# A transformer layer on one core: the first stage in another order, with column sums in place of row sums and twenty identity matmuls at the start

## The reference, cut to what matters

```python
mod = silu(c) @ w_ada + b_ada                      # 1024 -> 6 x 1024
sh_a, sc_a, g_a, sh_f, sc_f, g_f = split(mod)
h = layer_norm(x) * (1 + sc_a) + sh_a              # x: 512 x 1024
na_q, na_k, na_v, d_q, d_k, d_v = split(h @ w_in)  # 1024 -> 6 x 512
mix = concat(neighbourhood_attention(na_q, na_k, na_v, na_rpb),    # 8 heads
             diff_attention(d_q, d_k, d_v, t5_bias, lambdas)) @ w_out  # 4 heads
x = layer_norm(alpha * x + (1 + g_a) * mix, ln1)
h = layer_norm(x) * (1 + sc_f) + sh_f
f = peer(h)      # 8 heads x 16 experts a token: rows gathered from expert_down, expert_up
x = layer_norm(alpha * x + (1 + g_f) * f, ln2)
```

## Time and profile before

| | us |
|---|---|
| median of 3 runs (1943.44 to 1948.09) | 1945.46 |
| the profiled execution, its own time | 1944.35 |
| its span, first to last instruction | 1942.6 |
| first projection matmul starts | 96.47 |
| last projection copied out, attention starts | 269.15 |
| first gather of both kinds | 609.38 |

### The profile page before, as it was taken

One profiled execution on the slowest core, in us unless ns is written; L12 is line 12 of the kernel. 1 busy time (PEld: TensorE's weight loads), 2 busy tenths in 40 slices (PEclk: granted clock), 3 DMA queues, 4 the chain that ended last, 5 costly groups with the idle time before them and its releaser, 6 DMA issues.

```text
span 1942.6 us, 14972 instructions
## 1 busy us (share of the span) xinstructions
PE 1537.7 (79%) x4570; PEld 687.8 (35%) x4570; DVE 1178.0 (61%) x2808; ACT 388.6 (20%) x955; POOL 984.3 (51%) x1065
## 2 busy tenths in 40 slices
PE   2599999999998777777777777777777777777777
PEld 1244446655996222222222222222222222222222
DVE  1844027758801677666777766776766776676642
ACT  1100025520112111221111221111321111221111
POOL 0000000000303777777777777777777777777772
PEclk9999989999998999999999999999999999999999
DMA  4965443022504999999999999999999999999994
GB/s 139 343 249 211 131 129 74 14 109 87 196 1 155 409 409 409 409 410 409 409 410 409 407 409 408 409 402 406 407 405 404 408 405 403 410 404 409 406 409 185
DMA packets 193334, 612.95 MB, mean 316 GB/s; under 512 B 30248, under 2 KB 30632, under 8 KB 192968
## 3 DMA queue, kind: packets, MB, share of 16 engines
q0 software_dynamic: 147456, 536.94, 69.6%
q1 hardware_dynamic: 45800, 75.06, 11.9%
HBM read 605.77 MB, written 6.16 MB: 315 GB/s over the span
## 4 chain that ended last, share of the span: by engine, by line
PE 25%; DMA 25%; DVE 24%; POOL 15%; issue 7%; SPq 2%; ACT 1%; POOLq 0%; DVEq 0%; PEldq 0%
DMA big<-in_expert_down,expert_idx 24%; PE pair L441 22%; DVE big L926 9%; POOL big L419 8%; POOL big L410 8%; PE pair L560 2%; SPq L295 1%; DMA big<-in_expert_up,expert_idx 1%; DVE big L733 1%; PE pair L504 1%; DVE big L863 1%; DVE big L846 1%; DVE big L867 1%; DVE big L868 1%; PE pair L544 1%
## 5 line engine op out<-in xcount | busy, mean ns | idle before, releaser
L560 PE MATMUL pair<-big 128*128 128x512 f32 x2048 | 999.9, 612 | 323.1 <-DMA big<-in_expert_up,expert_idx 288.4
L926 DVE CUSTOM_DVE_ANT_0 big<-big,pair 128x1024 f32<-128x1024 f32 x512 | 611.2, 1219 | 340.8 <-DMA big<-in_expert_down,expert_idx 339.5
L560 PEld LDWEIGHTS pair<-big 128*128 128x128 f32 x2048 | 349.0, 189 | 973.3 <-issue 858.3
L410 POOL DMA_INDIRECT big<-in_expert_down,expert_idx x512 | 484.7, 947 | 300.7 <-issue 119.9
L419 POOL DMA_INDIRECT big<-in_expert_up,expert_idx x512 | 483.6, 944 | 156.9 <-issue 147.1
L441 PE MATMUL pair<-big 128*128 128x128 f32 (+3 forms) x1704 | 421.9, 415 | 21.6 <-DVE big L733 13.2
L441 PEld LDWEIGHTS pair<-big 128*128 128x128 f32 (+2 forms) x1704 | 237.2, 193 | 166.1 <-issue 147.8
L398 POOL TENSOR_SCALAR small<-small 128x1 f32<-128x1 f32 (+1 forms) x16 | 3.6, 226 | 463.6 <-DVE small L806 350.7
L636 ACT ACTIVATE big<-big 128x16 f32<-128x16 f32 x32 | 6.9, 215 | 1026.0 <-DVE big L926 1026.0
L647 ACT ACTIVATE big<-ident,big 128x128 f32<-128x128 f32 x512 | 153.0, 387 | 16.1 <-DVE big L881 16.1
L629 ACT ACTIVATE big<-pair 128x512 f32<-128x512 f32 (+1 forms) x136 | 77.9, 591 | 323.1 <-PE pair L441 227.0
(11 more groups left out here) (111 smaller groups left out, 662.4 us busy)
## 6 DMA issues: line engine op xcount, KB each, us to landing
big<-in_w_ada SPq DMA_DIRECT2D x12, 2048.0 KB, 17.6
big<-in_w_in SPq DMA_DIRECT2D x6, 2048.0 KB, 15.5
big<-na_scr SPq DMA_DIRECT2D x8, 1024.0 KB, 10.6
big<-in_w_query SPq DMA_DIRECT2D x4, 2048.0 KB, 12.8
big<-in_expert_down,expert_idx POOLq DMA_INDIRECT x512, 11.8
big<-in_expert_up,expert_idx POOLq DMA_INDIRECT x512, 11.9
big<-in_w_out SPq DMA_DIRECT2D x2, 2048.0 KB, 10.6
x_sb<-in_x SPq DMA_DIRECT2D x1, 2048.0 KB, 7.9
```

The costliest lines, as they stand in the source:

```text
L410: nc.gpsimd.indirect_dma_start(downs[at % DOWN_SLOTS], None, expert_down[0], bass.IndirectOffsetOnAxis(expert_idx[:, at:at + 1], 0)).then_ ...
L560: last = nc.tensor.matmul(pair[t % 2][:, s * HALF:(s + 1) * HALF], diag[:, at % TOPK, :], ups[:, at % UP_SLOTS, s * HALF:(s + 1) * HALF], ...
L926: v.tensor_tensor_reduce(out=downs[slot], in0=downs[slot], in1=u_cur[:, :], scale=1.0, scalar=0.0, op0=ALU.mult, op1=ALU.add, accum_out=do ...
```

## The change

It rewrites the first stage and leaves the rest as it is.

- SP starts c, the first 2048 values of the bias `b_ada` and `na_rpb` first, each as plain rows, then x, the tables and the keys, and at once five weight chunks; the lambda vectors and `subln` come behind these. PE transposes the rows (groups `cols`, `rpb_cols`) and DVE copies them out.
- PE begins with twenty matmuls of the identity with itself (`WARM`).
- DVE takes the statistics of all four tiles in a row, POOL the power for all four in one instruction; ACT writes the normalised tiles.
- Scale and shift are applied after the transpose, where they are one number for each partition: `h_act` and `h_dve` are eight groups, one for each 128 columns of x, emptied by ACT (3) and DVE (5) with scale and shift in the same instruction.
- So ada 0 to 3 need not be put on all partitions: `mod_columns` turns each sum into columns by matmuls with one column of `ones`. Of chunks 2 and 3 POOL sums three of the eight blocks (`sum_blocks`), in `tensor_scalar` and `tensor_tensor`.
- `t5_line` becomes two groups in place of eight (the four heads share one matmul) and goes, with `keys_t`, behind the first projection. The projections come in the order 2, 5, 3, 4, 0, 1.
- The transfers to `na_scr` and `t5_scr` (the latter in four parts) stand behind the load of chunk 9.

```diff
+IN_ORDER = [2, 5, 3, 4, 0, 1]
+WARM = 20
+ADA_ON_DVE = [KB, KB, 5, 5]
...
-    g += [("t5_line", (h, s)) for h in range(DIFF_HEADS) for s in range(2)]
-    g += [("keys_t", ())]
-        if n == ADA_FIRST - 1:
-            g += [("h_t", (t, s)) for t in range(TILES) for s in range(2)]
+    g = [("cols", ()), ("rpb_cols", ())]
+    g += [("na_table", (j,)) for j in range(8)]
+    g += [("h_act" if k % 3 == 1 else "h_dve", (k,)) for k in range(KB)]
+        if n == 0:
+            g += [("t5_line", (s,)) for s in range(2)]
+            g += [("keys_t", ())]
...
+            for n in range(WSLOTS, WSLOTS + 3):
+                load_chunk(n)
+            for n in range(WSLOTS + 3, WSLOTS + 5):
+                load_chunk(n)
             sp.wait_ge(act_evac, EVAC[INDEX[("na_table", (7,))]][1])
             sp.dma_start(bass.AP(na_scr, 0, [[GRID_W, NA_HEADS * RPB_R], [NA_HEADS * RPB_R * GRID_W, GRID_W],
...
+            def sum_blocks(n):
+                pool.wait_ge(w_in_slot[n], 16)
+                acc, w, k0 = pool_sum[:, n % 2, :], w_slot[n], ADA_ON_DVE[n]
+                link(nc.gpsimd.tensor_scalar(acc, w[:, k0, :], c_exp[:, k0:k0 + 1], None, ALU.mult))
+                for k in range(k0 + 1, KB):
+                    link(nc.gpsimd.tensor_scalar(pool_tmp, w[:, k, :], c_exp[:, k:k + 1], None, ALU.mult))
+                    last = nc.gpsimd.tensor_tensor(acc, acc, pool_tmp, ALU.add)
...
+            def mod_columns(n):
+                pe.wait_ge(ada_summed, n + 1)
+                if ADA_ON_DVE[n] < KB:
+                    pe.wait_ge(pool_summed, sum(k < KB for k in ADA_ON_DVE[:n + 1]))
+                for b in range(4):
+                    last = nc.tensor.matmul(mod_ps[:, 4 * n + b:4 * n + b + 1], first_sum[:, n, b * P:(b + 1) * P],
+                                            ones[:, 0:1], start=True, stop=(ADA_ON_DVE[n] == KB))
...
+            for _ in range(WARM):
+                nc.tensor.matmul(spare_bank[:, 0:P], ident[:, :], ident[:, :], start=True, stop=True)
...
+                if kind == "h_dve" and args[0] == 6:
+                    for n in range(ADA_FIRST):
+                        last = mod_columns(n)
+                    last.then_inc(mod_summed, 1)
...
+                if kind == "na_table" and args[0] == 4:
+                    act.wait_ge(shift_ready, 1)
+                    for t in range(TILES):
+                        nc.scalar.activation(x_norm[:, t, :], x_sb[:, t, :], ACT.Identity, bias=shift4[:, t:t + 1],
+                                             scale=rstd4[:, t:t + 1]).then_inc(norm_ready, 1)
...
+                    v.tensor_scalar(h_t[:, k, :], ps[:, :], mod_cols[:, KB + k:KB + k + 1], mod_cols[:, k:k + 1],
+                                    ALU.mult, ALU.add).then_inc(dve_evac, 1)
```

More of the change, by code:

```diff
@@ L101 @@
 INDEX = {g: i for i, g in enumerate(GROUPS)}
-ON_DVE = ("ada", "scores", "values", "out")
+ON_DVE = ("cols", "rpb_cols", "h_dve", "ada", "scores", "values", "out")
 def at_head(a, head):
@@ L204, in build @@
         gate_sum = misc[:, 3808:3810]
[L205 removed]
+        c_col = cols[:, 0:KB]
         c_exp = small[:, 8:16]
@@ L284, in _ @@
         def _(sp):
+            sp.dma_start(rows_nat[0:KB, :], c.rearrange("a (k p) -> (a k) p", p=P)).then_inc(cols_in, 16)
+            sp.dma_start(rows_nat[KB:3 * KB, :], b_ada[0, 0:2 * D].rearrange("(k p) -> k p", p=P)).then_inc(cols_in, 16)
+            sp.dma_start(rpb_nat, na_rpb[0].rearrange("h r c -> (h r) c")).then_inc(rpb_in, 16)
             sp.dma_start(x_sb[:, :, :], x[0].rearrange("(t p) d -> p t d", p=P)).then_inc(x_in, 16)
[L286 to L298, removed]
+            sp.dma_start(na_place_sb, na_place).then_inc(place_in, 16)
+            sp.dma_start(t5_place_sb, t5_place).then_inc(t5_in, 16)
+            sp.dma_start(t5_lhs, t5_bias).then_inc(t5_in, 16)
+            sp.dma_start(keys_nat, sub_keys[0].rearrange("a n k -> n a k")).then_inc(keys_in, 16)
             def chunk_used(n):
                 kind, i = STREAM[n]
-                if kind == "ada":
+                if n < ADA_FIRST:
+                    sp.wait_ge(mod_summed, 1)
+                elif kind == "ada":
                     sp.wait_ge(ada_summed, i + 1)
@@ L326, in _ @@
               .then_inc(na_written, 16)
[L327 to L330, removed]
+            sp.wait_ge(act_evac, EVAC[INDEX[("t5_line", (1,))]][1])
+            for q in range(4):
+                sp.dma_start(bass.AP(t5_scr, q * (P // 4) * (D + 1), [[P * (D + 1), DIFF_HEADS], [D + 1, P // 4], [1, D]]),
+                             t5_line).then_inc(t5_written, 16)
+            for n in range(WSLOTS + 5, CHUNKS):
                 load_chunk(n)
@@ L401, in _ @@
                 n += 1
+                if n == 1:
+                    pool.wait_ge(c_ready, 1)
+                    for i in range(ADA_FIRST):
+                        if ADA_ON_DVE[i] < KB:
+                            sum_blocks(i)
             def gather_down(head, j):
@@ L442, in product @@
                 return last
+            def mod_columns(n):
[5 more added lines that the diff above has]
+                                            ones[:, 0:1], start=True, stop=(ADA_ON_DVE[n] == KB))
+                    if ADA_ON_DVE[n] < KB:
+                        last = nc.tensor.matmul(mod_ps[:, 4 * n + b:4 * n + b + 1], pool_sum[:, n % 2, b * P:(b + 1) * P],
+                                                ones[:, 0:1], start=False, stop=True)
+                return last
@@ L737, in sum_chunk @@
                 last.then_inc(ada_summed, 1)
-            sum_chunk(0)
+            for n in range(ADA_FIRST):
+                sum_chunk(n)
+            dve.wait_ge(mod_summed, 1)
+            v.tensor_tensor(mod_cols[:, 0:KB], mod_ps[:, 0:KB], cols[:, KB:2 * KB], ALU.add)
+            v.scalar_tensor_tensor(out=mod_cols[:, KB:2 * KB], in0=mod_ps[:, KB:2 * KB], scalar=1.0,
+                                   in1=cols[:, 2 * KB:3 * KB], op0=ALU.add, op1=ALU.add).then_inc(mod_ready, 1)
+            dve.wait_ge(mod_ready, 1)
```

212 lines of the change are left out of this document (131 added, 81 removed).

## The result

| | us |
|---|---|
| kernel before, median of 4 runs (1943.44 to 1948.09) | 1946.45 |
| changed kernel, median of 4 runs (1923.16 to 1927.49) | 1925.92 |
| ratio, with its 95% interval | 0.9897 (0.9883 to 0.9912) |
| profiled execution of the changed kernel: its time, its span | 1925.01, 1923.1 |
| forecast, range | 1902, 1891 to 1914 |

The kernel became 20.5 us faster where 43.7 were forecast. The sign was right, the size was not, and the time lies outside the range.

A forecast was written before the change was run, and what follows sets the result against it. PE was taken to bound the kernel up to the first gathers, transfers after them. An earlier first projection gains 48.4 us, less 2.3 and 2.4: 43.7; 1944.35 becomes 1900.7, plus 1.1 gives 1902 us, range 1891 to 1914.

The forecast's parts named there:

- T: Start of the first projection on PE, 96.5 us in the kernel before; forecast at 48.1, so 48.4 us gone.
- the loads and the start of DVE: Before the sums: `t5_bias` lands at 12.8 us, DVE's statistics follow, and the first sum starts at 21.3.
- T, POOL: POOL's three blocks of ada chunks 2 and 3: 5.8 us a chunk, ending at 41.1, just behind DVE's 40.2.
- the upper bound: POOL's high estimate in the sums: 1.6 us a `tensor_scalar` at 512 columns, 11.5 us a chunk, adding 11.4 us.
- The first rival: In the sums, POOL and DVE shut each other out, or POOL is slow: T = 58.8, time 1913; chance 0.25.
- The late chunk: Table writes ahead of chunk 10 delay the third projection: margin 4.5 us, else PE stands 10 us, time 1911; chance 0.07.
- The clock: At the first projection PE's clock is down after thin work: 2.4 us lost, with ends 0 and 5.
- The T5 groups and the keys: Two `t5_line` groups and the keys, now on PE's path in the projections, add 2.3 us.
- the two rivals: POOL and DVE hindering each other or POOL slow (1913, chance 0.25), and chunk 10 late (1911, chance 0.07).
- The twenty matmuls: Identity matmuls at PE's start, meant for the clock: change nothing at T; without them the same time within 1 us.
- What came after attention began: Attention, output and gathers: unchanged work, only shifted; attention 44 us earlier, at 225, the gathers at 566.
- the rival with a slower kernel: POOL's additions in the sums take 102 us each, four 408: T = 485, time near 2338; chance 0.02.

The follow-up runs named there:

- the combined kernel with identities: Changed kernel with all sums by DVE, `t5_scr` by head, chunks 10 and 11 before table writes, identity matmuls in PE's waits; 3.0 and 1.5 us faster than without these identities.

## Why the prediction was wrong

**T, the loads and the start of DVE: right within 1.6 us.** The weights were issued at 4.50 instead of 35.62; DVE's statistics began at 14.4 (12.8 worked out), the first sum at 22.5 (21.3). The power took 1.05 us with four columns.

**T, POOL: the wrong size.** The failed term is "3 x 0.9 + 2 x 1.4 + gaps" = 5.8 us a chunk. Alone it is 7.6: 1.56 for a `tensor_scalar`, not 0.9, and 1.26 for a `tensor_tensor`, not 1.4. I took the growth of fill and select over 128 columns because they were nearer in width, and left the growth of the very operation, 2.7 ns a column and 1.6 us at 512, to the upper bound; that one was right. Chunk 2 landed at 30.7 instead of 29.5 (+1.2), POOL alone is 3.6 us longer over both chunks, running beside DVE adds 2.1: 6.9 of the 7.9 us. The columns took 3.7 instead of 3.0 and the copies 4.2 instead of 4.0.

**The first rival was true in part.** It was given as exclusion by instruction, 10.7 us later. POOL's slowness was the larger part for the end of the sums and hindrance the smaller, though hindrance is what made the division of work a loss.

**The late chunk: the step that failed.** It was named as a rival, with the right place, queue and sign, at 0.07. Its margin of 4.5 us rested on 6.1 us for `t5_scr`, from the earlier trace rows: a transfer of 128 partitions with four rows each. The new transfers have 4 heads as the outermost dimension, which the row of SP's order showed (`4x32x1024`; the one before is `128x4x1024`), and I read only their bytes. `na_scr` landed at T + 49.7, near the T + 47.5 of the sum. From there `t_scr` and chunk 10 took 28 us where I had 6.1 + 5.4, chunk 10 landed at T + 77.6 instead of T + 59, and PE stood 14.3 us, beyond even the 10 of the rival. The rival had put those 10 on `na_scr`; that was not where they came from. By my own margin, anything above 6.1 + 4.5 = 10.6 us was enough to stall. The 6.1 is also short for the new cut with all engines busy: at its 206 to 250 GB/s 2 MB need 8 to 10 us (an estimate), and PE still waited 3.5.

**The clock.** At T it was down for 5.2 us, as forecast: 2.6 us lost against 2.4. That the stall would bring it down a second time, at 133.8 us, was not in the rival's price; it cost another 3.2. PE did 6 records in 5.2 us there, and the clock was not fully up until a little later:

```profile
56.00:61.20 5.20, 5.20 (x6) 0.50 1.05 394
...
133.80:139.00 5.20, 5.20 (x6) 0.50 1.04 394
```

**The T5 groups and the keys: right.** With the clock up, from the first projection to attention PE takes 174.8 us (the combined kernel with identities) against 172.7 before: 2.1 us for them, 2.3 worked out.

**The range.** It took the two rivals one at a time, each to 1911 to 1913. They are independent, and both came: 1902 + 7.9 + 14.3 + 3.2 is 1927.4, 1.5 us above the measured median. A range over several independent risks has to reach over two of them together when their sum lies outside.

**The twenty matmuls** changed nothing within the noise, as forecast; the run without them shows it. **What came after attention began** was carried through as assumed, 18.1 us at the start of attention and 19.5 at the end. One price does not come out of its own terms: four additions of 102 us in place of 1.4 give T = 451 and not the 485 of the rival with a slower kernel. Nothing measured bears on it, since no POOL instruction of the sums took more than 2.05 us.

## What to carry to other kernels

Price a moved or rewritten transfer by its shape, outermost dimension first, and not by its bytes alone; a write that nobody waits for can still starve the queue behind it. Before a helper engine gets a share of the work, compare its time for one block with that of the engine it relieves, and count what the two do to each other: here 1.56 and 1.26 us against 0.78. And when a change of many parts gains half of what is expected, run its cheapest part alone: here one load written differently gave as much as the whole.

## What the runs showed of the hardware

- A store with dimensions 4 x 32 x 1024 kept 0.24 to 0.27 of the transfer engines busy, at 57 to 103 GB/s; the same data cut so that 32 is outermost kept 0.98 to 0.99 busy, at 206 to 250 GB/s.
- POOL on 128 x 512 f32 from SBUF: 1.56 us for a `tensor_scalar`, 1.26 for a `tensor_tensor` with two inputs; the instruction with one input is the slower one. Beside DVE they were 1.6 to 2.05 and 1.49.
- DVE's `scalar_tensor_tensor` with two operands from SBUF went from 0.78 to 1.15 us beside POOL, its `tensor_scalar` from 0.48 to as much as 1.49.
- The forty records of identity matmuls took 7.05 us from 1.77. They ran at 7 a microsecond up to 6.8 us and at 12 after it, while the column of the granted clock reads 1.00 from the start: this early it does not show the lower level, the record lengths do. In 12 to 28 us it reads 0.55; PE was 14.53 of the 16 us busy, nearly all with matmuls that use 32 of 128 rows, and the clock did not rise until the transposes over all rows, which begin at 27.4.
- From the start of attention to the first query product PE took 199.4 us where the clock was up in its first 17 us, and 202.5 to 207.8 where it was down there for part or all of the time (the same matmuls).
